# A hybrid encoder trunk on one core: fewer score matmuls, moved waits, and a weight sum formed by an adding transfer

## What is computed

```python
qkv = x @ w_qkv                      # q, k: 8 heads x 2 x 128; v: 8 heads x 256
s = einsum('bqhjd,bkhjd->bhjqk', q_blk, k)        # q scaled by 128 ** -0.5
p = softmax(where(allowed, s, -inf))              # block-causal mask of 64 rows
w = p[:, :, 0] - lam_full * p[:, :, 1]
o = einsum('bhqk,bkhe->bqhe', w, v)
y = (rms_norm(o, subln) * (1.0 - lam_init)).reshape(B, S, 2048) @ w_o
```

## Time and profile before

| | |
|---|---|
| time, median of 3 (lowest to highest) | 2125.41 us (2123.51 to 2125.71) |
| profiled execution | 2124.13 us, of it span 2122.4 us |
| mean granted clock of TensorE, share of full speed | 0.997 |
| PE busy | 2098.5 us (99%) |
| DVE busy | 1804.8 us (85%) |
| ACT busy | 1218.1 us (57%) |
| POOL busy | 197.9 us (9%) |
| loads issued by SP (queue 1) | 408.58 MB, 54.3% of 16 engines' span |
| transfers issued by POOL (queue 0) | 82.58 MB, 21.5% |

### The profile page before, as it was taken

One profiled execution on the slowest core, in us unless ns is written; L12 is line 12 of the kernel. 1 busy time (PEld: TensorE's weight loads), 2 busy tenths in 40 slices (PEclk: granted clock), 3 DMA queues, 4 the chain that ended last, 5 costly groups with the idle time before them and its releaser, 6 DMA issues.

```text
span 2122.4 us, 26845 instructions
## 1 busy us (share of the span) xinstructions
PE 2098.5 (99%) x10900; PEld 1802.4 (85%) x10900; DVE 1804.8 (85%) x1547; ACT 1218.1 (57%) x1097; POOL 197.9 (9%) x160
## 2 busy tenths in 40 slices
PE   9998999999999999999999999999999999999999
PEld 8787888898888888888898888889888888888887
DVE  6786557979989989889787888798888989989888
ACT  5554445456666666566546566545656666566563
POOL 0000030210000000000030013103000000000000
PEclk9999999999999999999999999999999999999999
DMA  9576446579889888898855777875789889898884
GB/s 315 153 218 217 138 167 211 180 242 270 251 239 261 248 272 248 230 289 244 276 171 198 203 218 221 269 241 201 229 239 261 254 249 259 240 290 239 228 247 178
DMA packets 244313, 493.78 MB, mean 233 GB/s; under 512 B 7968, under 2 KB 8224, under 8 KB 242912
## 3 DMA queue, kind: packets, MB, share of 16 engines
q1 hardware_dynamic: 205216, 408.58, 54.3%
q0 software_dynamic: 38400, 82.58, 21.5%
q10 hardware_dynamic: 576, 0.92, 0.1%
HBM read 489.95 MB, written 2.10 MB: 232 GB/s over the span
## 4 chain that ended last, share of the span: by engine, by line
PE 96%; DVE 1%; DMA 1%; issue 1%; ACT 1%; POOL 0%; SPq 0%; DVEq 0%; ACTq 0%
PE ps L802 56%; PE ps L1038 9%; PE ps L1036 9%; PE ps L1042 9%; PE ps L1137 2%; PE ps L1194 1%; PE ps L1199 1%; PE ps L1192 1%; PE ps L1460 1%; PE ps L1458 1%; PE ps L1465 1%; PE ps L1444 1%; PE ps L1438 1%; PE ps L1440 1%; PE ps L879 1%
## 5 line engine op out<-in xcount | busy, mean ns | idle before, releaser
L802 PE MATMUL ps<-X,hi 128*128 128x512 f32 (+1 forms) x3008 | 703.0, 379 | 14.9 <-issue 7.7
L802 PEld LDWEIGHTS ps<-X,hi 128*128 128x128 f32 x3008 | 553.7, 190 | 117.7 <-issue 16.0
L1857 ACT ACTIVATE hi<-raw 128x2048 fp32r<-128x2048 f32 x196 | 372.6, 1915 | 234.0 <-DVE raw L2707 150.8
L2267 DVE TENSOR_TENSOR lo<-raw,hi 128x2048 fp32r<-128x2048 f32 x210 | 476.5, 2287 | 24.9 <-PE ps L1042 10.5
L802 PE MATMUL ps<-X,lo 128*128 128x256 f32 x2816 | 387.5, 283 | 0.0
L802 PEld LDWEIGHTS ps<-X,lo 128*128 128x128 f32 x2816 | 372.7, 191 | 12.1
L2267 DVE TENSOR_TENSOR lo<-up_raw,hi 128x2048 fp32r<-128x2048 f32 x120 | 274.3, 2286 | 38.7 <-PE ps L802 38.7
L1547 ACT ACTIVATE hi<-raw 128x2048 fp32r<-128x2048 f32 x102 | 193.8, 1913 | 103.8 <-PE ps L802 61.7
L2149 DVE TENSOR_TENSOR lo<-raw,hi 128x2048 fp32r<-128x2048 f32 x88 | 201.5, 2300 | 46.8 <-ACT hi L1547 40.7
L1841 ACT ACTIVATE hi<-up_raw 128x2048 fp32r<-128x2048 f32 x112 | 214.2, 1913 | 24.2 <-PE ps L1042 11.2
L1038 PE MATMUL ps<-hi,forms 128*128 128x512 f32 x448 | 175.5, 392 | 0.0
(11 more groups left out here) (331 smaller groups left out, 2924.2 us busy)
## 6 DMA issues: line engine op xcount, KB each, us to landing
raw<-in_mlp_w_dram SPq DMA_DIRECT2D x144, 1024.0 KB, 7.7
up_raw<-in_mlp_w_dram SPq DMA_DIRECT2D x112, 1024.0 KB, 7.7
raw<-in_mlp_w_dram POOLq DMA_DIRECT2D x56, 1024.0 KB, 9.4
raw<-in_gla_w_in_dram SPq DMA_DIRECT2D x48, 1024.0 KB, 5.5
raw<-in_attn_w_qkv_dram SPq DMA_DIRECT2D x39, 1024.0 KB, 5.2
raw<-in_attn_w_o_dram SPq DMA_DIRECT2D x16, 1024.0 KB, 5.2
raw<-in_gla_w_o_dram SPq DMA_DIRECT2D x16, 1024.0 KB, 6.5
up_raw<-in_attn_w_qkv_dram SPq DMA_DIRECT2D x8, 1024.0 KB, 7.2
```

Source lines behind the costliest of these rows:

```text
L802: return pe.matmul(o, w, m, start=start, stop=stop)
L1857: act.activation(hi[:, P_AT[p] % 4], raw[:, slot], ACT.Copy).then_inc(hi_ready, 2 if p == PRODUCTS - 1 else 1)
L2267: dve.tensor_tensor(lo[:, at % 3], src, hi[:, at % 4].bitcast(F32), ALU.subtract).then_inc(lo_ready, n)
```

## The change

- **Scores.** k's low and high part lie side by side in `k_parts`. One matmul of q's high part now covers both (256 or 512 columns), and a second one adds q's low part by k's high part: four matmuls for each of two maps where there were six. The result has two halves, the product with k's low part and the rest, in three banks, `FIRST_AT` and the two of `SCORES_AT`. `softmax_max` first adds the mask to the first half (four more DVE instructions and one more wait), then adds the other and takes the maximum as before.
- **Waits.** The waits for `halves_added` 10, 12 and 14 and for `v_added` 9 move from the head of a group into it, behind its first tile, where a bank of the other four is first written.
- **Second sum.** `unit_sum(u, 2)` goes. POOL issues `second_sum(u)`, a transfer that reads the same weight quarter again from HBM and adds it into the tile, once the low part of product 1 is made. It stands behind `third_sum(u)` and ahead of `rms_power` and `fourth_sum`. ACT's high part of product 2 waits for its landing.
- **Order.** In unit 0 `v_form_sums(1)` goes ahead of `unit_up_lo(0, 0)`, `v_form_high(1)` and `v_form_low(1)` go late, `squares` and `normalise` and `unit_hi(0, 3)`, `unit_lo(0, 3)` move. In unit 1 `v_add(1, 5)` goes ahead of `qk_low(3)`. The first low parts of unit 0 wait for one tile less of `w_used`.
- **Start.** POOL issues its four small transfers only when all of x is transposed and split (`x_lo` 8).

```diff
+FIRST_AT = (5, 4, 4, 5)
-        k_lo = nc.alloc_sbuf_tensor_at("k_lo", [P, 4, SEQ], F32R, offset=work_at + 4 * 1024)
-        k_hi = nc.alloc_sbuf_tensor_at("k_hi", [P, 4, SEQ], F32R, offset=work_at + 4 * 2048)
+        k_parts = nc.alloc_sbuf_tensor_at("k_parts", [P, 2, 4, SEQ], F32R, offset=work_at + 4 * 1024)
+        k_lo, k_hi = k_parts[:, 0], k_parts[:, 1]
...
             def third_sum(u):
-                pool.wait_ge(v_w_summed, 2 * u + 1)
+                pool.wait_ge(v_w_summed, u + 1)
...
+            def second_sum(u):
+                t, c = KPT * (2 * u + 1), 2 * D + COLS
+                pool.wait_ge(lo_ready, 4 * G_UNIT[u] + P_AT[1] + 1)
+                pool.dma_start(raw[:, first_slot(u)], w_qkv[:, t:t + KPT, c + COLS:c + 2 * COLS], accum_op=ALU.add
+                               ).then_inc(v_w2_added, 16)
...
+            pool.wait_ge(x_lo, 8)
             pool.dma_start(lam_rows.rearrange("p a b -> p (a b)"),
...
             third_sum(0)
+            second_sum(0)
             rms_power(0, 0)
             rms_power(1, 1)
             fourth_sum(0)
             third_sum(1)
+            second_sum(1)
             fourth_sum(1)
...
-                    for rows, keys, at in ((blk(0), blk(0), slice(0, P)), (blk(1), slice(0, SEQ), slice(P, P + SEQ))):
-                        acc = ps[:, SCORES_AT[c][s], at]
-                        mm(acc, q_hi[:, i, rows], k_hi[:, i, keys], True, False)
-                        mm(acc, q_lo[:, i, rows], k_hi[:, i, keys], False, False)
-                        m = mm(acc, q_hi[:, i, rows], k_lo[:, i, keys], False, True)
+                    first = ps[:, FIRST_AT[c], s * SEQ:(s + 1) * SEQ].rearrange("p (a t) -> p a t", a=2)
+                    mm(first, q_hi[:, i, blk(0)], k_parts[:, :, i, blk(0)], True, False)
+                    mm(first[:, 1, :], q_lo[:, i, blk(0)], k_hi[:, i, blk(0)], False, True)
+                    second = ps[:, SCORES_AT[c][s], :].rearrange("p (a t) -> p a t", a=2)
+                    mm(second, q_hi[:, i, blk(1)], k_parts[:, :, i, :], True, False)
+                    m = mm(second[:, 1, :], q_lo[:, i, blk(1)], k_hi[:, i, :], False, True)
...
             def scores_of(c):
+                free = (v_added, 9) if c == 1 else (halves_added, 12)
+                return {(0, 1): lambda: (pe.wait_ge(*free), scores(2 * c, 0, c)), ...
             def outputs_of(c):
+                free = 2 * (2 * c + 3)
+                return {(0, 1): lambda: (pe.wait_ge(halves_added, free), weigh_values(2 * c, 0, c), ...
...
             pe.wait_ge(halves_added, 8)
-            pe.wait_ge(v_added, 9)
             cols_group(G_Q[2], 0, X, scores_of(1))
             pe.wait_ge(maxes, 16)
             pe.wait_ge(mixedT_ready, 4)
-            pe.wait_ge(halves_added, 10)
             cols_group(G_K[2], 1, X, outputs_of(1))
             pe.wait_ge(o_lo, 4)
-            pe.wait_ge(halves_added, 12)
+            pe.wait_ge(halves_added, 10)
             cols_group(G_Q[3], 0, X, scores_of(2))
             pe.wait_ge(maxes, 24)
             pe.wait_ge(mixedT_ready, 6)
-            pe.wait_ge(halves_added, 14)
+            pe.wait_ge(halves_added, 12)
             cols_group(G_K[3], 1, X, outputs_of(2))
...
+                elif p == 2:
+                    act.wait_ge(v_w2_added, 16 * u + 16)
...
             copy_mixedT(0, 0)
-            v_form_high(1)
             unit_hi(0, 0)
             copy_v(1, (w_used, 4 * G_V[0] + 4), v_rows[:, 1, :])
             unit_up_hi(0, 1)
-            unit_hi(0, 1)
             copy_mixedT(1, 1)
             squares(0, 0)
+            unit_hi(0, 1)
+            squares(1, 1)
             unit_up_hi(0, 2)
-            squares(1, 1)
             unit_hi(0, 2)
-            unit_hi(0, 3)
+            v_form_high(1)
             o_hi_head(0, 0)
             o_hi_head(1, 1)
             keep_v(0, 0, BANK)
             keep_v(1, 1, BANK + 1)
+            unit_hi(0, 3)
...
+                for s in range(2):
+                    dve.tensor_tensor(probs[:, s, 0:P], first[:, s, 0, :], mask[:, 0:P], ALU.add).then_inc(low_scores, 1)
+                    dve.tensor_tensor(probs[:, s, P:], second[s][:, 0, :], mask[:, P:], ALU.add).then_inc(low_scores, 1)
+                dve.wait_ge(low_scores, 4 * n + 4)
...
-                dve.wait_ge(w_used, 4 * g + at - 2)
+                dve.wait_ge(w_used, 4 * g + at - (3 if g == G_UNIT[0] and at < 3 else 2))
...
             mix_maps(0, 0)
+            v_form_sums(1)
             unit_up_lo(0, 0)
             softmax_max(1, 1)
-            v_form_sums(1)
             mix_maps(1, 1)
             unit_lo(0, 0)
             unit_sum(0, 1)
-            v_form_low(1)
             unit_up_lo(0, 1)
             unit_lo(0, 1)
-            unit_sum(0, 2)
             normalise(0, 0)
+            normalise(1, 1)
             unit_up_lo(0, 2)
-            normalise(1, 1)
             unit_lo(0, 2)
-            unit_lo(0, 3)
             o_lo_head(0, 0)
             o_lo_head(1, 1)
+            unit_lo(0, 3)
+            v_form_low(1)
...
             unit_lo(1, 1)
-            unit_sum(1, 2)
...
             unit_lo(1, 6)
+            dve.wait_ge(v_added, 5)
+            v_add(1, 5, 2, 1)
             qk_low(3, kT, k_hi, k_lo)
             late_lo(G_Q[2], 0, -2)
-            dve.wait_ge(v_added, 5)
-            v_add(1, 5, 2, 1)
             late_lo(G_Q[2], 1, 0)
```

More of the change, by code:

```diff
@@ L343, in build @@
         pairs_seen = sem("pairs_seen")
+        low_scores = sem("low_scores")
         maxes = sem("maxes")
@@ L363, in build @@
         v_w_summed = sem("v_w_summed")
+        v_w2_added = sem("v_w2_added")
         v_w3_added = sem("v_w3_added")
@@ L1101, in scores_of @@
             def scores_of(c):
-                return {(0, 1): lambda: scores(2 * c, 0, c), (1, 0): lambda: scores(2 * c + 1, 1, c),
+                free = (v_added, 9) if c == 1 else (halves_added, 12)
+                return {(0, 1): lambda: (pe.wait_ge(*free), scores(2 * c, 0, c)), (1, 0): lambda: scores(2 * c + 1, 1, c),
                         (2, 0): lambda: turn_mixed(2 * c, 0), (3, 0): lambda: turn_mixed(2 * c + 1, 1)}
             def outputs_of(c):
-                return {(0, 1): lambda: (weigh_values(2 * c, 0, c), weigh_values(2 * c + 1, 1, c)),
+                free = 2 * (2 * c + 3)
+                return {(0, 1): lambda: (pe.wait_ge(halves_added, free), weigh_values(2 * c, 0, c), weigh_values(2 * c + 1, 1, c)),
                         (2, 0): lambda: (turn_output(2 * c, 0), turn_output(2 * c + 1, 1))}
@@ L1680, in unit_hi @@
                     act.wait_ge(raw_full[slot], 16 * LOADED_UNIT[u] + 16)
-                elif p in (1, 2):
-                    act.wait_ge(v_w_summed, 2 * u + p)
+                elif p == 1:
+                    act.wait_ge(v_w_summed, u + 1)
+                elif p == 2:
+                    act.wait_ge(v_w2_added, 16 * u + 16)
                 elif p == 4:
@@ L2199, in softmax_max @@
                 dve.sem_inc(scores_seen, 1)
+                b0, b1 = SCORES_AT[n // 2]
+                first = ps[:, FIRST_AT[n // 2], :].rearrange("p (s a t) -> p s a t", s=2, a=2)
+                second = [ps[:, b, :].rearrange("p (a t) -> p a t", a=2) for b in (b0, b1)]
+                for s in range(2):
+                    dve.tensor_tensor(probs[:, s, 0:P], first[:, s, 0, :], mask[:, 0:P], ALU.add).then_inc(low_scores, 1)
+                    dve.tensor_tensor(probs[:, s, P:], second[s][:, 0, :], mask[:, P:], ALU.add).then_inc(low_scores, 1)
+                dve.wait_ge(low_scores, 4 * n + 4)
+                dve.sem_inc(scores_seen, 1)
                 for s in range(2):
@@ L2202, in softmax_max @@
                         i = 2 * s + t
-                        dve.tensor_tensor_reduce(probs[:, s, a:b], ps[:, SCORES_AT[n // 2][s], a:b], mask[:, a:b], 1.0, MASKED,
+                        dve.tensor_tensor_reduce(probs[:, s, a:b], second[s][:, 1, :] if t else first[:, s, 1, :],
+                                                 probs[:, s, a:b], 1.0, MASKED,
                                                  ALU.add, ALU.max, row_max[:, i:i + 1]).then_inc(maxes, 1)
```

## The result

The changed kernel takes 2106.7 us (median of 4, 2106.2 to 2107.6) beside 2124.9 us for the kernel before on the same chip; the ratio is 0.991, with an interval of 0.990 to 0.993. The profiled execution took 2106.17 us, its span 2104.4 us (before: 2124.13 and 2122.4). The forecast was 2106.0 us.

What follows compares the result with a forecast made beforehand. TensorE was taken as the bound: its work plus its pauses. Terms -7.8 - 12.6 + 5.0 - 1.3 - 1.0 = -17.7 us took 2124.1 to 2106 us; the range was 2099 to 2114.

Steps and rivals of the forecast that it cites:

- Moved waits, -20.4 us: Heads of G_Q[2], G_K[2], G_Q[3], G_K[3]: four PE pauses and their lower clock go, 7.8 and 12.6 us.
- Scores, -1.3 us, and maxima: Attention: four matmuls save 0.22 us a call, six calls counted; longer maxima cost nothing in the later pairs.
- Landing of unit 1, 12.0 us: Second sum in unit 1 queues behind the third, lands at 154.5; high part ready at 156.4.
- its rival of 9.3 us: Unit 1: second sum lands after 9.3 us, unit costs 0.8 instead of 5.0 us, total 2102; chance 0.27.
- held-up descriptors: Both units: DVE's work delays adding transfers, second sums land 9 us later than forecast, about 2130 us; chance 0.03.
- +5.0 us: Unit 1 ends 5.0 us late, as product 2 waits for the second sum; bounds 0.5 and 9.
- the pause lies between those of 2.97 and 4.89 us: Unit 1, product 2: those pauses cost 1.6 and 2.7 us of clock, so this one costs 1.7.
- Unit 0, 0.8 us gained: Unit 0: two pauses go, product 2 waits 1.4 us anew; some 0.8 us of gain left when unit 1 starts.
- Unit 0 ends later than before: Unit 0: a listed sign that would show the prediction wrong.
- Start, -1.0 us: Kernel start: later small transfers cut PE's 1.31 us wait; 1.0 us gained, between 1.8 gained and 1.0 lost.
- The pause at 82.79: Unit 0: the pause stays, since `v_form_sums(1)` and longer maxima fill what the low part's earlier start gives.
- pause 1: Head of G_Q[2], PE waiting for the last addition into v: 5.1 us idle plus 2.7 of clock, 7.8 gained.

Runs made afterwards that it cites:

- e3_small_early: The changed kernel with POOL issuing the small transfers at once, as before, not behind `x_lo` 8: 2110.5 us.
- e6_act_order: The changed kernel with ACT's forms, heads and `keep_v` of unit 0 ahead of the high part of product 2: 2104.6 us.
- e12_adding_unit1: The changed kernel with the adding transfer for the second sum in unit 1 alone, unit 0's sum formed by DVE: 2102.9 us.
- e2_dve_sums: The changed kernel with the second sum of both units formed by DVE again, behind the low part of product 1: 2098.3 us.
- e5_second_first: The changed kernel with POOL issuing `second_sum` ahead of `third_sum` in both units: 2101.1 us.
- e9_dve_early: e2_dve_sums with the small transfers issued at once, as before the change: 2101.2 us.
- e8: e2_dve_sums with the scores and maxima of before for the first pair of heads alone: 2096.6 us.
- e1: The kernel before with only PE's waits for `v_added` 9 and the halves moved behind the first tile of their groups: 2104.2 us.
- e11: The changed kernel with the adding transfer for the second sum in unit 0 alone, unit 1's sum formed by DVE: 2102.7 us.
- e13: The changed kernel with second sum ahead of third in both units and ACT's unit 0 forms, heads and `keep_v` ahead of product 2's high part: 2099.6 us.

## Why the prediction was right

The mechanism held: the pauses behind the moved waits went as worked out, and the second sum of unit 1 landed behind the third. The time was 0.7 us off, and that it came so close is luck: terms were mis-sized on both sides and cancelled.

- **Moved waits, -20.4 us: right.** Alone they gave 21.5. In the change the low products of G_Q[2] begin at 179.69, after a unit that ends 3.3 us later and with its pause gone: 4.5 us ahead of before, forecast 3.8. The cover held as worked out:

```profile
180.34 0.69 DVE L2311 TENSOR_TENSOR v_unit_rows<-v_unit_rows,ps 128x512 f32<-128x512 f32 x1
...
181.60 0.28 PE L815 MATMUL ps<-k_parts,q_hi 128*128 128x256 f32 x1
182.19 0.28 PE L815 MATMUL ps<-k_parts,q_hi 128*128 128x256 f32 x1
...
183.14 0.29 DVE L2220 TENSOR_TENSOR work<-ps,work 128x128 f32<-128x128 f32 x1
185.71 0.17 DVE L2231 TENSOR_SCALAR neg_max<-row_max 128x4 f32<-128x4 f32 x1
```

  The last addition ends at 181.0, 0.6 us ahead of the scores.
- **Scores, -1.3 us, and maxima: right in the trace.** The maps stand 0.59 us apart (0.58 forecast, 0.69 before); the six calls are worth 1.25 us. In the three later pairs a maximum takes 2.6 us to its negation (2.5 forecast) and costs PE nothing. Of the 1.25 us 0.45 is given back at 1185 to 1331 us; "behind 345 us nothing changes" was wrong by that much.
- **Landing of unit 1, 12.0 us: right; at 154.5 and PE at 156.4: luck.** It took 11.9 us. That it came at 154.29, and PE at 156.34, agrees by chance: the forecast's times leave out the gain at the start and have 0.8 gained in unit 0, and in the trace the 2.1 us of the start were nearly used up ahead of unit 1, by 0.5 and 1.0 us. The reading of `ln_g` and `ln_b`, two transfers of one queue that pass one after the other, carried over, and the forecast beat its rival of 9.3 us. The issue took 1.28 us while DVE worked, so the case of held-up descriptors did not come either.
- **Unit 1: too much.** The +5.0 us hold the 0.8 gained in unit 0, so unit 1 by itself was put at 5.8 us; from its first tile to its third it takes 3.9 more than before (31.45 and 27.58). PE waits 3.3 us for product 2 where 3.7 was forecast, and the 1.7 us for the clock were not lost in this execution. In e3_small_early, e6_act_order and e12_adding_unit1 the clock did fall at that place, for 1.1 to 1.2 us. The step that failed is "the pause lies between those of 2.97 and 4.89 us": a pause's length doesn't decide it.
- **Unit 0, 0.8 us gained: mis-sized.** From the tile at 81.24 to unit 1 the kernel takes 49.65 us, before 48.63: one us lost. The waits of 0.57 and 2.31 us went as forecast; e2_dve_sums, without the transfer, takes 45.31. The landing took 10.1 us, not 9.2, since the third sum, issued 6.6 us ahead, is still in the queue (8.4 us without it, e5_second_first); the pause was 2.48 us, not 1.4; and 1.6 us of clock, which I had not counted there, went behind it. "Unit 0 ends later than before" was a sign of being wrong; it ends at 130.89 us beside 131.42, but only by the gain at the start, without which it would be 1.6 us late.
- **Start, -1.0 us: too little.** 2.1 in the trace, and the last small transfer, issued at 27.55 us, landed after 6.4 us, in time. I counted only the wait of 1.31 us less its doubt; the two waits for ACT's high parts before it came back with it in e9_dve_early (0.81 and 0.16 us), so they belong to the small transfers too. PE's pauses there are 0.37 and 0.48 us where under 0.3 was forecast.
- **The pause at 82.79: partly right.** It grew from 0.44 to 1.42 us, where I had it stay. The new additions are 2.4 us of DVE there, and e8 shows them to be its cause.

The sum by the traces, with the forecast in brackets: start -2.1 (-1.0), tile at 81.2 +0.5 (0), unit 0 +1.0 (-0.8), unit 1 +3.9 (+5.8), pause 1 -7.9 (-7.8), the other three pauses -12.6 (-12.6), scores -1.25 (-1.3), second layer +0.45 (0). That is -18.0, the difference of the spans, beside -17.7. The start and unit 1 came out 3.0 us better than forecast, the tile, unit 0 and the second layer 2.75 us worse.

What the prediction did not ask is whether the transfer is worth having. It costs 8.4 us and saves DVE 2.3 us a unit, which DVE idles away waiting for it.

## What to carry to other kernels

Before an engine's work is handed to a transfer, compare the two latencies on the chain that waits: here 2.3 us of an engine with idle time behind it against 8.5 us at best, and 12 when a transfer of the same queue goes ahead. Where one is used, the one that is needed first is issued first, and whatever does not depend on it goes ahead of its consumer in the queue of the engine that waits. A wait for a buffer belongs at the first instruction that writes that buffer: this alone gave more than the whole change. Time saved early in such a chain need not reach the end: here small waits of PE far behind the change took back 0.4 to 0.7 us of it.

## What the runs showed of the hardware

- **The lower clock behind a pause comes in some executions and not in others.** It fell behind pauses of PE of 2.32 us (e1), 2.48 (the change), 2.97 twice, 3.11 (e12), 3.84 (e3), 3.91 (e6) and 4.89 us; it stayed at 2.4 GHz behind 2.19 (e11), 2.31, 2.52 (e3), 2.81 and 3.18 us (the change). The pair of 2.31 and 2.32 us has the same instructions around it. A fall to 1.2 GHz costs 1.6 us behind the pauses of 2.32, 2.48 and 2.97 us and 1.1 to 1.2 us behind those of unit 1 (3.11, 3.84, 3.91). Not all of it need last: of the 1.6 us of the change 0.8 is left at the head of unit 1, against e3. What decides a fall was not found; the length of the pause alone does not.
- **Adding transfers of 1 MB on one queue pass one after the other.** The second sum lands after 8.4 to 8.5 us with none ahead (e5, e13), after 11.8 to 11.9 when issued 4.4 us behind the third, and after 9.7 to 10.1 when 6.6 us behind. The third lands after 8.7 to 9.9 us with none ahead and after 12.7 to 13.3 when issued 0.8 us behind the second.
